# Decoder step on one core: feed-forward in three weight passes, sample-group steps moved behind the token mix, a one-instruction silu gate

## The reference

```python
mod = c_act @ P['w_ada'][l] + P['b_ada'][l]
sh1, sc1, g1, sh2, sc2, g2 = ...
h = rmsnorm(x, P['g_norm1'][l]) * (1.0 + sc1) + sh1
mix, states = token_mix(h, ...)        # w_in, then HGRN2 | Mamba-2 | RWKV-7 heads, then @ w_out
x = x + (g1 * mix)
h = rmsnorm(x, P['g_norm2'][l]) * (1.0 + sc2) + sh2
ff = (jax.nn.silu(h @ P['w_gate'][l]) * (h @ P['w_up'][l])) @ P['w_down'][l]
x = x + (g2 * ff)
y = rmsnorm(x, P['g_final'])
```

## Time and profile before

| what | us |
|---|---|
| median of 3 runs | 1936.76 |
| lowest, highest run | 1924.67, 1938.64 |
| the profiled execution | 1930.92 |
| its span, first to last instruction | 1929.1 |

### The profile page before, as it was taken

The page is one execution under the profiler, slowest core; times in us unless marked ns, Lnnn a source line. Parts: engine busy times, 40 slices in busy tenths (PEclk is TensorE's granted clock), DMA queues, the critical chain, the costliest instruction groups (busy, mean ns, idle before and its releaser), DMA issues.

```text
span 1929.1 us, 32185 instructions
## 1 busy us (share of the span) xinstructions
PE 1645.1 (85%) x13599; PEld 1489.4 (77%) x13599; DVE 979.2 (51%) x2112; ACT 587.4 (30%) x1055; POOL 256.1 (13%) x333
## 2 busy tenths in 40 slices
PE   4899998888998185778788887999969999999995
PEld 2898887777886143457677787988969999999995
DVE  5414447776553456766766535555552332423334
ACT  2313233323331321233443333334332222222222
POOL 3501111111000312123233440000000000000000
PEclk9899999889998566668889998999989999999998
DMA  8111011111100433432112243343312231322211
GB/s 302 44 48 30 24 29 35 41 41 43 48 34 9 156 99 125 151 96 74 53 39 83 76 136 91 105 123 103 113 50 66 64 99 45 100 64 68 84 49 55
DMA packets 199302, 149.23 MB, mean 77 GB/s; under 512 B 6479, under 2 KB 187200, under 8 KB 198136
## 3 DMA queue, kind: packets, MB, share of 16 engines
q1 hardware_dynamic: 188482, 120.67, 20.8%
q0 software_dynamic: 7728, 23.27, 3.5%
q10 hardware_dynamic: 2950, 3.24, 0.5%
HBM read 134.03 MB, written 13.18 MB: 76 GB/s over the span
## 4 chain that ended last, share of the span: by engine, by line
PE 69%; DVE 18%; ACT 6%; issue 3%; DMA 2%; POOL 0%; SPq 0%; POOLq 0%; DVEq 0%; ACTq 0%
PE bank L1261 17%; PE bank L1262 17%; PE bank L1263 17%; PE bank L1200 3%; ACT WHI L1825 1%; PE bank L1652 1%; PE bank L1653 1%; PE bank L1488 1%; PE bank L1487 1%; PE bank L1433 1%; PE bank L1426 1%; PE bank L1283 1%; PE bank L1435 1%; PE bank L1584 1%; PE bank L1403 1%
## 5 line engine op out<-in xcount | busy, mean ns | idle before, releaser
L1261 PE MATMUL bank<-HBH,WHI 128*128 128x328 f32 (+1 forms) x832 | 261.1, 314 | 14.8 <-DVE HBL L2384 10.1
L2267 DVE TENSOR_TENSOR WLO<-RAW,WHI 128x1024 fp32r<-128x1024 f32 (+4 forms) x149 | 152.3, 1025 | 235.9 <-ACT WHI L1825 235.4
L1825 ACT CAST WHI<-RAW 128x1024 fp32r<-128x1024 f32 (+4 forms) x210 | 187.9, 898 | 245.3 <-PE bank L1263 237.0
L1262 PE MATMUL bank<-HBL,WHI 128*128 128x328 f32 (+1 forms) x832 | 259.6, 312 | 0.0
L1263 PE MATMUL bank<-HBH,WLO 128*128 128x328 f32 (+1 forms) x832 | 258.7, 311 | 0.0
L1261 PE MATMUL bank<-HHI,WHI 128*128 128x344 f32 x568 | 190.5, 335 | 10.3 <-DVE HLO L2480 6.2
L1022 POOL TENSOR_TENSOR WLO<-RAW,WHI 128x1024 fp32r<-128x1024 f32 (+1 forms) x61 | 131.6, 2159 | 456.0 <-ACT WHI L1825 456.0
L1262 PE MATMUL bank<-HLO,WHI 128*128 128x344 f32 x568 | 184.3, 324 | 0.0
L1263 PE MATMUL bank<-HHI,WLO 128*128 128x344 f32 x568 | 184.2, 324 | 0.0
L1261 PEld LDWEIGHTS bank<-HBH,WHI 128*128 128x128 f32 x832 | 157.1, 189 | 16.0 <-issue 15.8
L1263 PEld LDWEIGHTS bank<-HBH,WLO 128*128 128x128 f32 x832 | 157.3, 189 | 0.0
(11 more groups left out here) (579 smaller groups left out, 3199.1 us busy)
## 6 DMA issues: line engine op xcount, KB each, us to landing
RAW<-in_w_gate SPq DMA_DIRECT2D x44, 512.0 KB, 3.9
RAW<-in_w_up SPq DMA_DIRECT2D x44, 512.0 KB, 3.9
RAW<-in_w_ada SPq DMA_DIRECT2D x32, 512.0 KB, 4.1
RAW<-in_w_in SPq DMA_DIRECT2D x26, 512.0 KB, 3.8
ADAW<-in_w_ada SPq DMA_DIRECT2D x8, 1024.0 KB, 19.9
RAW<-in_w_out SPq DMA_DIRECT2D x16, 512.0 KB, 4.4
RAW<-in_w_down SPq DMA_DIRECT2D x32, 256.0 KB, 2.7
RAW<-in_w_down SPq DMA_DIRECT2D x16, 384.0 KB, 3.5
```

Source lines behind the costliest of these rows:

```text
L1261: mm(bank[:, 0:w], whi[:, k, :], hi_k, start=(k == 0), stop=False)
L1262: mm(bank[:, 0:w], whi[:, k, :], lo_k, start=False, stop=False)
L1825: a.copy(w_split(i)[0][:, 0:nk, :], RAW[u % NRAW][:, 0:nk, :]).then_inc(w_hi, 1)
L2267: v.tensor_tensor(wlo[:, 0:nk, :], RAW[u % NRAW][:, 0:nk, :], whi[:, 0:nk, :].bitcast(F32), ALU.subtract).then_inc(w_lo, 1)
```

## The change

1. **Three passes.** The feed-forward runs chunk by chunk: out, gate, up and down of chunk 0, then of chunk 1, then of chunk 2, each with its own load and split of every weight. Groups are 4, 4, 4, 4, 3, 3 for chunk 0 and 6, 6, 5, 5 for chunks 1 and 2. The `out` units of chunk 1 stand between the groups of chunk 0 (three after each group from the third on), those of chunk 2 in the third group of chunk 1. The first pair of the next group stands ahead of the `down` units of a group (in chunks 1 and 2, and at the end of chunk 0). Norms are cut in halves and put between units (`later`).
2. **Split lead.** Weights are split two units ahead of use before the barrier and, behind it, three units ahead of the one whose product is taken out (`emit`), with three slots of WHI and WLO behind the barrier where there were two for chunk 0 and four in PLAN3.
3. **Samples.** None of the SAMPLES stands in the token mix any longer. They stand behind `join`, one after each 12 x 384 columns of matmul work, and the long ones are cut in two (sr6b, sr7b, sh6b, sm4b, sm5b), 37 steps in all. Their state buffers lie in memory that is free only behind the barrier, and two states share one buffer with the loads of the third. Their PSUM bank is bank 6. `mixsplit` for chunk 0 no longer waits for the states.
4. **Gate.** From the third group of chunk 0 on (gate 8, quantum QJ) a gate is one silu on ScalarE; the two groups before it keep exp, ln, exp. ScalarE then has both table sets in use in this stretch, and `tables` loads the one that a step needs.
5. **y.** y tiles 0 to 2 and 3 to 4 are brought out inside the passes of chunks 1 and 2; 5 to 8 at the end. From QJ on six PSUM banks turn for the quanta.

```diff
-GROUPS = [[4, 4, 4, 4, 3, 3], [6, 6, 5, 5]]
+GROUPS = [[4, 4, 4, 4, 3, 3], [6, 6, 5, 5], [6, 6, 5, 5]]
+AFTER = 2
-NORMS = [3, 6, 4, 5, 7, 8]
+NORMS = [3, 4, 6, 5, 7, 8]
...
     def chunks(u):
-        return range(NCH) if u < N1 else (0,) if u < N2 else (1, 2)
+        return range(NCH) if u < N1 else (UNITS[u][1][0],)
...
+    for c in (1, 2):
+        begun, end = 1, 0
+        for g, n in enumerate(GROUPS[c]):
+            end += n
+            ahead = min(end + 1, FF // P)
+            units += pairs(c, begun, ahead)
+            begun = ahead
+            if c == 1 and g == 2:
+                units += out[2]
+            elif c == 1 and g == len(GROUPS[c]) - 1:
+                units += pairs(2, 0, 1)
+            units += downs(c, g)
...
-            b = 3 if q < QP2 else (2, 3, 7)[(q - QP2) % 3] if q < QP2A else q % 7
+            b = 3 if q < QP2 else (2, 3, 7)[(q - QP2) % 3] if q < QJ else q % 6
...
     def evac_engine(q):
         kind = UNITS[QUANTA[q][0]][0]
-        return 'dve' if kind in ('out', 'up', 'down') or (kind == 'gate' and QUANTA[q][1] == 0) else 'ada' if kind == 'ada' else 'act'
+        if kind == 'gate':
+            return 'dve' if q < QJ else 'act'
+        return 'dve' if kind in ('out', 'up', 'down') else 'ada' if kind == 'ada' else 'act'
...
+        def emit(item):
+            PLAN2.append(item)
+            upto = n1s
+            if item[0] == 'half' and item[1][1] != 0 and not joined:
+                upto = SIDX[UNITS_OF(item[1][0])] + 2
+            elif item[0] == 'ev' and joined:
+                upto = SIDX[UNITS_OF(item[1])] + 3
...
                 PLAN2.append(item)
-                if samples and item[0] != 'mb_out':
-                    PLAN2.append((samples.pop(0), 0))
...
+            if item[0] == 'half':
+                u, c = QUANTA[item[1][0]]
+                spent += unit_k(u) * FCW[c]
+            if samples and spent >= 12 * FCW[0]:
+                PLAN2.append((samples.pop(0), 0))
+                spent = 0
...
                     if arg == 0:
-                        act.wait_ge(hgs_out, 16)
-                        act.wait_ge(ssms_out, 32)
-                        act.wait_ge(wkv_out, 16)
+                        act.wait_ge(ada_turned, 3)
...
                 elif what == 'sm9':
+                    tables(LN_EXP)
                     act.wait_ge(*ms_at('pe')('ssq'))
                     ssq_scale(NS, S, SRM, 256).then_inc(ms_act, 1)
```

More of the change, by code:

```diff
@@ L135, in dense_plan, with pairs, downs @@
     n1 = len(units)
[L136 to L146, removed]
+    out = [[('out', (c, t)) for t in range(KT)] for c in range(NCH)]
+    def pairs(c, f0, f1):
+        return [(kind, (c, f)) for f in range(f0, f1) for kind in ('gate', 'up')]
+    def downs(c, g):
+        return [('down', (c, g, d)) for d in range(KT)]
+    units += out[0]
+    f = 0
+    for g, n in enumerate(GROUPS[0]):
+        units += pairs(0, f, f + n)
+        f += n
+        if g >= AFTER:
+            units += out[1][3 * (g - AFTER):3 * (g - AFTER) + 3]
+        if g == len(GROUPS[0]) - 1:
+            units += pairs(1, 0, 1)
+        units += downs(0, g)
+    for c in (1, 2):
[10 more added lines that the diff above has]
+            units += downs(c, g)
+    return units, n1
 def kernel_program(nc, ins, outs):
@@ L827, in kernel_program @@
                 ffn.append(('half', (q, None)))
-            if q - 1 >= QP2 and q - 1 != LASTQ[N1 + 7] and UNITS_OF(q - 1) not in up_ends:
-                ffn.append(('ev', q - 1))
-            if UNITS_OF(q) in up_ends:
-                ffn += [('ev', q), ('pause', 0)]
-            if q == LASTQ[N1 + 7]:
-                ffn += [('ev', q), ('sum', 3), ('pause', 0), ('scaled', 3), ('pause', 0), ('rest', 3), ('pause', 0)]
-        ffn.append(('ev', QP2A - 1))
+            queued.append(q)
+            while queued and (queued[0] < q or unit in NOW):
+                done = queued.pop(0)
+                ffn.append(('ev', done))
+                if later:
+                    item = later.pop(0)
+                    ffn += [item] if item else []
+                later += EARLY.get(UNITS[UNITS_OF(done)], [])
+            ffn += NOW.get(unit, [])
+        assert not later
+        ffn += [('ev', len(QUANTA) - 1), ('sum', 8), ('normed', (8, 0)), ('normed', (8, 1))] + [('y', i) for i in range(5, 9)]
+        NEXT = [n1s + 2]
+        joined = []
+        def emit(item):
[5 more added lines that the diff above has]
+                upto = SIDX[UNITS_OF(item[1])] + 3
+            while NEXT[0] <= min(upto, len(SPLIT) - 1):
+                PLAN2.append(('split', NEXT[0]))
+                NEXT[0] += 1
         def fill(n, whole=False):
-            while ffn and n >= 0:
+            while ffn and n >= 0 and ffn[0][0] != 'stop':
                 if ffn[0][0] == 'pause':
@@ L871, in kernel_program @@
                         PLAN2.append(('adt', 2))
-        assert not late and not samples
+        assert not late
         PLAN2.append(('mix_final', 0))
@@ L1241, in dense @@
                 if kind == 'down':
-                    tiles = sum(GROUPS[arg[0]][:arg[1] + 1])
-                    pe.wait_ge(gu_lo, tiles if c == 0 else FF // P + 2 * (tiles - 1) + c)
+                    tiles = range(FIRST_F[c][arg[1]], FIRST_F[c][arg[1]] + GROUPS[c][arg[1]])
+                    pe.wait_ge(gu_lo, UP_AT[(c, tiles[-1])] + 1)
                 if u < N1:
@@ L1248, in dense @@
                 elif kind == 'down':
-                    src = [gcols(c, k) for k in range(unit_k(u))]
+                    src = [gcols(c, gate_slot(c, f)) for f in tiles]
                     w = FCW[c]
@@ L1748, in mix_final, with y_last @@
                 last.then_inc(fin_pe, 1)
+            def y_last(i):
+                n = BLK if i < NB else NS
+                pe.wait_ge(n_h, 6 + NORMS.index(8) + 1)
+                if i < 7:
+                    for e in EV:
+                        pe.wait_ge(evac[e], sum(q <= len(QUANTA) - 3 for q in EV[e]))
+                else:
+                    pe.wait_ge(y_act, i - 1)
+                    pe.wait_ge(y_dve, i - 1)
+                t, t0 = xtile(i)
+                for k in range(KT):
+                    last = turn(BK8[YB[2 * (i % 2) + k // 4]][0:n, (k % 4) * P:(k % 4 + 1) * P], t[:, k, t0:t0 + n], P)
+                last.then_inc(y_turned, 1)
             for what, arg in PLAN2:
```

398 lines of the change are left out of this document (204 added, 194 removed).

## The result

Four runs of the changed kernel have a median of 1901.99 us (1899.52 to 1906.85), the kernel before in the same comparison 1933.51. The ratio is 0.9842 with a 95% interval from 0.982 to 0.9865: some 31 us faster, where the forecast, 1866, was some 67. The direction and the places were right, but less than half of the gain came.

A forecast was written before the change was run, and what follows sets the result against it. TensorE was taken as the bound, never resting from 1450 to 1850 us, with time to gain before and at the end. 1103 + 174.4 + 527.1 + 14 + 22 + 20.6 + 1.3 = 1862.4, forecast 1866; own range 1850 to 1884.

The forecast's parts named there:

- the 40 us of the token mix: Blocks 0 to 2 without samples: 30.6 from block 1, 3.3 from block 0, 6 for small steps' trips; bounds 27 and 50.
- Blocks 3 to 7, 5 more: Split now ahead of bringing out the product, so gate instructions stand before the next block step; 5 us more, at most 13.
- Behind gate 8, 737.5: From gate 8 to the last unit's end: matmuls of 174.4 and 527.1, other matmuls 14, uncovered waits 22 us.
- Other matmuls: On TensorE: transposes of the last x tile and y, five sums, some 70 small sample matmuls; 14 us (8 to 20).
- What stays uncovered: Waits left behind gate 8: sample steps, norms of chunks 1 and 2, barrier and tile changes; 22 us, bounds 8 and 60.
- (a): At sr12, sh10 and sm9, ScalarE's small-matmul wait, table loads and gate delay a split; 2.7 us lost three times, 8.
- (b): Chunk 1's norm, 16 VectorE instructions with sh6 between them, falls among short down units; 7 us.
- The end: Last unit follows directly, 11 us less; the 20.6 after it stays, plus 1.3 for a table load.
- Chains win: Rival: ScalarE waits in more of the 37 steps, 16 steps at 2.4 us more, giving 1904; chance 0.15.
- The ring of loads: Rival: weight-tile loads become the bound; 18 us at 8.5 us landing, slower than before from 9.9; chance 0.04.
- A table switch above its load: Rival: each table switch holds ScalarE 1.28 us longer than its load, adding 13 us, giving 1879; chance 0.03.
- the last rival: Change gives nothing: token mix bound otherwise, half of 57 us of waits come back, giving 1928; chance 0.03.

The follow-up runs named there:

- a_repeat: The changed kernel run once more with nothing changed, beside the others; median 1900.7 us, ratio 0.9815 to the kernel before.
- a_evfirst: The changed kernel with the old order in blocks 3 to 7, product brought out before the split; 1890.0 us, ratio 0.9768.
- a_best5: Changed kernel with old order in blocks 3 to 7, samples placed aside, early exp table, regrouped tiles, GpSimd's three state waits moved ahead of the first y tile; 1887.9 us.
- a_short: The changed kernel with the samples' 24 long VectorE instructions cut to 64 elements a partition in place of 1024; 1888.7 us, ratio 0.9761.
- a_expgate: The changed kernel with exp, ln, exp in place of silu for all gates of chunk 0, 14 more of them; 1918.1 us, ratio 0.9916.

## Why the prediction was right and wrong

Two steps of the sum failed most: the 40 us of the token mix, and the stretch behind gate 8, where the waits were too low and the wider distances of the matmuls stood at nothing. Against a_repeat (span 1896.8) the forecast's sum of 1862.4 is 34.4 us short, and the table says where: 2.9 ahead of block 0 (not the kernel's), 10.1 in blocks 0 to 2 (5.5 to 13.1 by the other profiles of that code), 4.7 up to gate 8, 14.3 behind it, 2.4 in the tail.

- **Token mix, 40 less:** it was 30. The step that failed is "30.6 + 3.3 + 6". Without samples blocks 0 to 2 take 133.4, between 43 and 46 each. So block 1 had 29.3 us of samples (73.3 to 44.0) and not 30.6, block 0 had nothing to give (46.0 and 46.2); and the 6 us for the trips of small steps weren't there. My lower bound, 27, was nearer.
- **Blocks 3 to 7, 5 more:** 9.7, of which the swapped order is 6.1, shown by a_evfirst, by another mechanism than the one I named (the wait in front of WHI and not the gates' instructions). Some 3 us are left in every three-pass kernel; their cause stays open.
- **Behind gate 8, 737.5:** 751.8. The matmuls at full clock were right, 701.5. "Other matmuls" were 10.1 and not 14. "What stays uncovered" was 26.7 and not 22. And a term stood at nothing: 13.5 us by which the matmuls stand further apart than 173 and 148.4 ns, 1.5 of it lower clock and 4.4 waiting that the profile hides at the last matmul before a wait. It is most of the 14.3. I had such a rest in the profile of before and misread it ("the rest is matmuls at the lower clock after such waits"): of those 18 us, 7.1 are the first 48 matmuls of chunks 1 and 2, which begin at 1344.1 and not at 1351.6, and 5.1 are lower clock.
- **The samples behind the barrier** are the reason why the waits were more. I priced them at 8 for (a) and some of the 14, and hid all long instructions; they cost 20.4. By its parts (a) was not too low: the waits at sr12, sh10 and sm9 add up to 4.6, and taking the tables away gave 3.9; the two waits at sm9, 1.5 us, stay without the tables. The failed sentence is "three at most (3.7 us) between two splits ... so they hide": three long instructions meet half a norm of 2.2 us in front of one split (5.9 us), as in the rows above, and the long ones cost 6.1. Then each small product stands on TensorE itself (4.9).
- **(b), 7 for the norm of chunk 1:** 5.9, the five waits from 1293.7 to 1315.9 in a_repeat, of which 4.0 also stand there without samples.
- **The end:** the table load added its 1.28 (1.4 measured, both without samples and by taking it away). The other 2.4 us lie behind the last copy of y, 6.2 us ahead of the end where it was 3.9, in all kernels with samples behind the barrier. GpSimd's waits were not the cause (a_best5). The records of the trace show what it is: GpSimd's last instruction but for semaphores, a drain, takes 3.00 us in these kernels and 0.79 in the kernel before and in all without samples. Why it takes longer stays open.
- **Rivals.** Chains win (1904) gave the right number, by a partly right mechanism: of its 38 us, 20 came, and a third of these were load and not chains. The ring of loads did not bound, but it came nearer: ScalarE waits 24.3 us for RAW behind gate 8 in a_repeat and 5.5 before, and of TensorE's waits only one of 0.2 us goes straight back to it; in a_best5 one of 2.4 us does. A table switch above its load did not happen. The 1928 of the last rival does not follow from its own words: half of 57 is 28.5, and a token mix that gives nothing takes back 40.

What the change was worth, by stretches that differ in one point of the change: the samples leave the token mix, -28.6; three passes in place of two, with the split lead and the order that belong to them, -32.8 (771.2 to 738.4, both without samples and with exp gates; TensorE's waits in it fall from 44.8 to 20.0); the silu gate, -7.0; the samples behind the barrier, +20.4; order and the open rest ahead of gate 8, +9.7; the tail, +3.7. The sum is -34.6, beside 31 to 34 by the two comparisons of medians (1933.5 and 1935.0 against 1902.0 and 1900.7). So the big move of the change, the samples, came to 8 us net, or 6 with the 2.4 that they cost in the tail (the medians say 25.5 against 19.6), and some 70% of its gain came back as waits, wider distances and TensorE's own work. The gain is the three passes.

## What to carry to other kernels

Work that is moved from a stretch with idle engines into one where the bound engine is full keeps its price: count its instructions on the bound engine itself, look for the one place where two moved things stand in front of the same split, and leave a term for what stands beside the waits (here 13.5 us beside 26.7). Before such a rest is called a lower clock, the granted clock has to be read for the stretch: here it was 1.5 of the 13.5. An operation that lets an engine go on without asking another is worth little alone and much where the other's queue has grown: the silu gate gave 0, 7 and 21 us in three surroundings. And before a stretch of two profiles is compared, compare one with the same code in both: here it moved by up to 16 us.

## What the runs showed of the hardware that was not expected

- The same instructions, 0 to block 0, took 677.5 to 693.2 us in the profiles of this study. The first 650 us of a_short, the fastest there, and of the changed kernel's first profile, the slowest (columns as in the earlier trace rows), have a granted clock of 0.94 and 0.92. The same 5273 matmuls keep TensorE busy for 542.9 and 558.3 us, 15.4 more, which is nearly all of the 15.7 between the two starts of block 0: the difference is its clock and not waits.

```profile
0.00:650.00 650.00, 542.90 (x5273) 478.91 (x5273) 331.71 (x748) 196.67 (x399) 112.61 (x215) 0.94 0.18 58
```

```profile
0.00:650.00 650.00, 558.33 (x5273) 491.76 (x5273) 330.81 (x746) 193.30 (x396) 100.26 (x194) 0.92 0.17 54
```

- Table loads of 1.28 us cost some 0.4 us each of the time behind gate 8, where ScalarE is busy for 41%; only the one at the end, on the chain of the last norm, cost all of it.
- GpSimd's closing drain took 3.00 us in every kernel with the sample steps behind the barrier and 0.79 in every other, on the path to the end.
- In a stretch of 752 us with 29 waits of up to 2.7 us (a_repeat) the granted clock fell once, for 3.4 us; with waits of up to 5.6 us (a_expgate) it was down for 20.5 us of 773.
